# A macaron transformer block on one core: adaLN sums along k with outputs on partitions, x also transposed by the host, a first phase in passes of k-tiles, weights laid out in long runs

## What is computed

```python
mod = silu(c) @ w_ada + b_ada                 # c: [1, D], w_ada: [D, 9 D]
sh1, sc1, gt1, sh2, sc2, gt2, sh3, sc3, gt3 = split(mod, 9)
u = rmsnorm(x, norm1_g) * (1 + sc1) + sh1
h = x + 0.5 * gt1 * swiglu(u, ffn1_w_in, ffn1_w_out)      # D -> 2 x 5632 -> D
u = rmsnorm(h, norm2_g) * (1 + sc2) + sh2
h = h + gt2 * mixer(u)                        # windowed attention + mLSTM, w_in, w_att_up, w_mlstm_up, w_out
u = rmsnorm(h, norm3_g) * (1 + sc3) + sh3
h = h + 0.5 * gt3 * swiglu(u, ffn2_w_in, ffn2_w_out)
out = rmsnorm(h, final_g)
```

## Time and profile before

| | us |
|---|---|
| median of 3 runs | 2054.93 |
| lowest, highest | 2054.68, 3204.81 |
| span of the profiled execution | 2052.8 |
| TensorE busy in it | 2030.3 (99%) |
| VectorE busy | 1735.4 (85%) |
| ScalarE busy | 1195.1 (58%) |
| DMA, mean over the span | 263 GB/s |

### The profile page before, as it was taken

How to read it: one execution, slowest core, us unless ns; L and a number is a source line. 1 busy time by engine, 2 the same in 40 slices (tenths; PEclk the granted TensorE clock), 3 DMA queues, 4 the chain that set the end, 5 groups by cost and what they waited for, 6 DMA issues and landing times.

```text
span 2052.8 us, 24243 instructions
## 1 busy us (share of the span) xinstructions
PE 2030.3 (99%) x9197; PEld 1674.2 (82%) x9197; DVE 1735.4 (85%) x2038; ACT 1195.1 (58%) x1668; POOL 4.5 (0%) x22
## 2 busy tenths in 40 slices
PE   7999999999999999999999999999999999999998
PEld 6888888888888888888777888888888888888887
DVE  6998998888889898887998898988778777787786
ACT  4667444655346565446545666567775477755764
POOL 0000000000000000000000000000000000000000
PEclk9999999999999999999999999999999999999999
DMA  9998899998999778985666687565565556565554
GB/s 371 387 387 321 328 334 338 343 336 315 327 341 336 269 261 326 334 299 181 218 217 211 230 298 278 204 216 195 186 240 191 202 185 204 206 205 192 177 200 149
DMA packets 249572, 540.80 MB, mean 263 GB/s; under 512 B 11888, under 2 KB 14320, under 8 KB 248688
## 3 DMA queue, kind: packets, MB, share of 16 engines
q1 hardware_dynamic: 248368, 539.11, 74.1%
q10 hardware_dynamic: 1088, 0.15, 0.0%
HBM read 537.10 MB, written 2.11 MB: 263 GB/s over the span
## 4 chain that ended last, share of the span: by engine, by line
PE 94%; DMA 2%; DVE 2%; issue 1%; ACT 0%; SPq 0%; ACTq 0%; DVEq 0%
PE pb L909 13%; PE pb L917 13%; PE pa L909 13%; PE pb L913 13%; PE pa L917 13%; PE pa L913 12%; PE pa L1064 2%; PE pa L1058 2%; PE pa L1061 2%; DMA raw<-in_ffn_w_in_dram 1%; PE pa L1228 1%; PE pb L1219 1%; PE pb L1224 1%; PE pb L1228 1%; PE pa L1219 1%; PE pa L1224 1%
## 5 line engine op out<-in xcount | busy, mean ns | idle before, releaser
L1494 ACT CAST hi<-raw 128x1024 fp32r<-128x1024 f32 (+2 forms) x662 | 682.2, 1035 | 704.8 <-PE pb L917 316.3
L2105 DVE TENSOR_TENSOR lo<-raw,hi 128x1024 fp32r<-128x1024 f32 (+2 forms) x662 | 784.0, 1199 | 230.5 <-ACT hi L1494 228.0
L2205 DVE SCALAR_TENSOR_TENSOR ada_acc<-ada_w,cond,ada_acc 128x1024 f32<-128x1024 f32 (+1 forms) x210 | 236.7, 1127 | 6.3
L909 PE MATMUL pa<-hi,act_hi 128*128 128x512 f32 x816 | 226.4, 394 | 0.0
L909 PE MATMUL pb<-hi,act_hi 128*128 128x512 f32 x816 | 221.0, 393 | 0.0
L917 PE MATMUL pb<-lo,act_hi 128*128 128x512 f32 x816 | 218.2, 389 | 0.0
L917 PE MATMUL pa<-lo,act_hi 128*128 128x512 f32 x800 | 217.8, 389 | 0.0
L913 PE MATMUL pb<-hi,act_lo 128*128 128x512 f32 x800 | 214.0, 389 | 0.0
L913 PE MATMUL pa<-hi,act_lo 128*128 128x512 f32 x736 | 200.3, 389 | 0.0
L917 PEld LDWEIGHTS pb<-lo,act_hi 128*128 128x128 f32 x816 | 153.2, 188 | 32.0
L909 PEld LDWEIGHTS pb<-hi,act_hi 128*128 128x128 f32 x816 | 151.8, 188 | 32.7 <-issue 2.2
(11 more groups left out here) (482 smaller groups left out, 2622.1 us busy)
## 6 DMA issues: line engine op xcount, KB each, us to landing
raw<-in_ffn_w_in_dram SPq DMA_DIRECT2D x155, 1024.0 KB, 5.4
ada_w<-in_w_ada_dram SPq DMA_DIRECT2D x207, 512.0 KB, 6.4
raw<-in_w_in_dram SPq DMA_DIRECT2D x63, 1024.0 KB, 5.3
raw<-in_ffn_w_out_dram SPq DMA_DIRECT2D x60, 1024.0 KB, 5.2
ada_s<-in_w_ada_dram SPq DMA_DIRECT2D x64, 512.0 KB, 11.6
pair<-in_ffn_w_in_dram SPq DMA_DIRECT2D x20, 1024.0 KB, 6.7
raw<-in_ffn_w_out_dram SPq DMA_DIRECT2D x24, 768.0 KB, 4.5
raw<-in_w_out_dram SPq DMA_DIRECT2D x16, 1024.0 KB, 5.1
```

Of the source, the lines that this page charges most:

```text
L909: pe.matmul(bank[:, tt, cols], a_hi[:, k0 + kk, tok], w_hi[:, kk, cols], start=start and kk == 0, stop=False, skip_group_check=on)
L1494: act.copy(hi_of(ph, i, j, half)[:, 0:n, 0:w], raw_of(ph, i, j)[:, 2 * half:2 * half + n, 0:w])\
L2105: dve.tensor_tensor(lo_of(ph, i, j)[:, s, 0:w], raw_of(ph, i, j)[:, s, 0:w], hi_of(ph, i, j, half)[:, 0:n, 0:w].bitcast(F32), ALU.subtract)\
L2205: ins = dve.scalar_tensor_tensor(out=acc, in0=wt, scalar=cond[:, kt:kt + 1], in1=acc, op0=ALU.mult, op1=ALU.add)
```

## The change

The host lays out the inputs anew: each weight matrix in blocks of 512 columns, so that one chunk gives every partition one run of 8 KB (2 KB before); ffn1_w_in again in the order of the first phase (`w_first`); w_ada transposed, [output on partitions, k]; x also transposed (`x_t`); c, the norms and b_ada as columns (`cols`).

**adaLN.** cond is spread over all partitions as a row (16 small matmuls, four copies by DVE). A tile is [128 outputs, k], and one instruction multiplies it by the row and sums along k (`accum_out`). A k-tile's shift and scale need two products of 2048 columns. All flushes, folds and sums on PE go (`start_flush`, `fold_rows`, `gate_sums`). Gate rows, GT1 too in four quarters, go through DRAM.

**First phase.** In passes over k-tiles (0, 1), (2, 3), (4 to 7), (8 to 11), (12 to 15). A pass has two halves: two groups g that stay in their banks from the pass before, then the other two. Four sets of banks: pa, pb, px, pq. x comes transposed; DVE multiplies by gain and the row of reciprocal roots (`start_mod`), ACT adds the shift to get act_hi. In ffn1_out0 the chunks come in forward order, and its gate tiles stand 2 to a chunk.

```diff
+PASSES = ((0, 1), (2, 3), (4, 5, 6, 7), (8, 9, 10, 11), (12, 13, 14, 15))
+def first_chunks():
+    out = []
+    for p, kts in enumerate(PASSES):
+        one, two = ((0, 1), (2, 3)) if p % 2 == 0 else ((2, 3), (0, 1))
+        if p < 3:
+            out += [(p, 0, [(kt, g, ab) for g in one for ab in (0, 1)]) for kt in kts]
+        else:
+            out += [(p, 0, [(kt, g, ab) for ab in (0, 1) for kt in kts[k:k + 2]]) for k in (0, 2) for g in one]
+        if p < 2:
+            out += [(p, 1, [(kt, g, ab) for ab in (0, 1) for kt in kts]) for g in two]
+        else:
+            out += [(p, 1, [(kt, g, ab) for kt in kts]) for g in two for ab in (0, 1)]
+    return out
...
-    ada_plan("ffn1_out0", [2, 1, 2, 1] * 4)
+    ada_plan("ffn1_out0", [2] * 11 + [1, 1, 0, 0, 0])
...
+    NEW = {kt: min(u for u in range(64) if kt in [b[0] for b in first_unit_of(u)[2]]) for kt in range(KD)}
+    S_AT = {0: (0, 0), 1: (1, 2), 2: (6, 7), 3: (8, 9), 4: (13, 14), 5: (16, 17), 6: (18, 19), 7: (20, 21),
+            8: (27, 28), 9: (29, 30), 10: (32, 33), 11: (34, 35), 12: (43, 44), 13: (45, 46), 14: (48, 49), 15: (50, 51)}
...
+            def load_start(kt):
+                for m in (SC1, SH1):
+                    k = 2 * kt + (m == SH1)
+                    if k >= S_RING:
+                        sp.wait_ge(s_dve, k - S_RING + 1)
+                    sp.dma_start(ada_s[:, k % S_RING, :], w_ada[m * KD + kt, :, :]).then_inc(ada_s_in[k % S_RING], 16)
...
+            sp.dma_start(c_in[:, :], c).then_inc(c_ok, 16)
+            for tt in range(TT):
+                sp.dma_start(h[:, tt, :], x[:, tt, :]).then_inc(x_in[tt], 16)
+            for pos in range(32):
+                ahead = pos + (pos >= 12)
+                while loaded < KD and NEW[loaded] // 2 <= ahead:
...
+                    load_start(loaded)
+                    loaded += 1
+                load(plan["ffn1_in0"], 0, pos, w_first[pos], 4)
                 load_ada(plan["ffn1_in0"].c0 + pos)
...
+                cond_rows()
+                keep_busy(8)
+                rstd_row()
+                keep_busy(24)
+                pe.wait_ge(cond_row_ok, 4)
+                pe.wait_ge(rs_ok, 1)
+                for u in range(64):
+                    if u == 57:
+                        pe.wait_ge(pa_free, 2)
+                        transposes(0)
+                    if u in (60, 63):
+                        nb = (u - 57) // 3
+                        pe.wait_ge(nat_lo, 2 * nb)
+                        transposes(nb)
+                    first_unit(ph, u)
...
+                def keep(p, g, ab, after):
+                    act.wait_ge(unit_used, after + 1)
+                    act.copy(part[:, g, ab, :, :], bank[:, :, :]).then_inc(part_ok if p > 0 else bank_ok, 1)
+                    if p > 0:
...
+                        act.copy(bank[:, :, :], part[:, other, ab, :, :]).then_inc(bank_ok, 1)
...
-                            ins = dve.scalar_tensor_tensor(out=acc, in0=wt, scalar=cond[:, kt:kt + 1], in1=acc,
-                                                           op0=ALU.mult, op1=ALU.add)
+                    dve.scalar_tensor_tensor(out=wt, in0=wt, scalar=1.0, in1=cond_row[:, half * ADA_W:(half + 1) * ADA_W],
+                                             op0=ALU.mult, op1=ALU.mult, accum_out=macc[:, half, col:col + 1])\
...
+            def start_tile(kt, m):
+                k = 2 * kt + (m == SH1)
+                dve.wait_ge(ada_s_in[k % S_RING], 16 * (k // S_RING + 1))
+                wt = ada_s[:, k % S_RING, :]
+                dve.scalar_tensor_tensor(out=wt, in0=wt, scalar=1.0, in1=cond_row[:, :], op0=ALU.mult, op1=ALU.mult,
+                                         accum_out=macc[:, 0, m * KD + kt:m * KD + kt + 1]).then_inc(s_dve, 1)
+            def start_mod(kt):
...
+                dve.tensor_tensor(mod[:, sh], macc[:, 0, sh], bada[:, sh], ALU.add)
+                dve.scalar_tensor_tensor(out=gain[:, kt:kt + 1], in0=macc[:, 0, sc], scalar=sc_bias[:, kt:kt + 1],
+                                         in1=par[:, PAR["g1"] + kt:PAR["g1"] + kt + 1], op0=ALU.add, op1=ALU.mult)\
+                    .then_inc(s_mod, 1)
...
+                dve.scalar_tensor_tensor(out=n_t[:, kt, :], in0=n_t[:, kt, :], scalar=gain[:, kt:kt + 1],
+                                         in1=rs_row[:, :], op0=ALU.mult, op1=ALU.mult).then_inc(x_t_ok, 1)
+            def start_lo(kt):
...
+                for u in range(64):
+                    for kt in range(KD):
+                        if S_AT[kt][0] == u and kt > 0:
+                            start_tile(kt, SC1)
+                        if S_AT[kt][1] == u:
+                            start_tile(kt, SH1)
+                            start_mod(kt)
+                    for kt in range(KD):
+                        if NEW[kt] == u:
+                            start_lo(kt)
...
                     split(ph, 0, u // 2, u % 2, 2)
```

More of the change, by code:

```diff
@@ L123, in build, with tile_col @@
     SH1, SC1, GT1, SH2, SC2, GT2, SH3, SC3, GT3 = range(9)
[L124 to L140, removed]
+    HALF_ROWS = [(GT1, q) for q in range(4)] + [(m, half) for m in (SH2, SC2, GT2, SH3, SC3, GT3) for half in (0, 1)]
+    ROWS_OUT = (GT1, GT2, GT3)
+    ROW_TILES = [8 if m == GT1 else 16 for m, _ in HALF_ROWS]
+    TILES = [(row, sub) for row in range(len(HALF_ROWS)) for sub in range(ROW_TILES[row])]
+    def tile_col(t):
+        row, sub = TILES[t]
+        m, part_ = HALF_ROWS[row]
+        return m * KD + part_ * (ROW_TILES[row] // 2) + sub // 2, sub % 2
     n_tiles = {}
@@ L177, in build @@
             ring_of[t] = (ring is gates_tiles, k % size, k // size, ring[k - size] if k >= size else None)
[L178 to L184, removed]
@@ L208, in s_used, with mod_after, mod_count @@
-    def s_used(q, n):
-        on_dve = sum(kt not in ON_PE[x // KD] for x in range(KD * q + n) for kt in (x % KD,))
-        return on_dve, KD * q + n - on_dve
+    MODS = [(GT1, q) for q in range(4)] + [(m, 1) for m in (SH2, SC2, GT2, SH3, SC3, GT3)]
+    def mod_after(t):
+        row, sub = TILES[t]
+        return HALF_ROWS[row] if sub == ROW_TILES[row] - 1 and HALF_ROWS[row] in MODS else None
+    def mod_count(m, part_=1):
+        return MODS.index((m, part_)) + 1
+    S_RING = 4
+    FIRST = first_chunks()
@@ L602, in tile_in @@
             return (gate_in if late else ada_in)[slot], turn
-        def tile_sum(row, w):
-            return gate_acc[:, 0:w] if HALF_ROWS[row][0] == GT3 else ada_acc[:, row % 2, 0:w]
         def over(eng, n, body):
@@ L987, in gate_sums @@
[L987 to L997 removed]
+                    pe.transpose(px[:, 0, 0:P], ident[:, :], ident[:, :])
@@ L1145, in out_phase @@
                     for j, half, k0, n in units(4, kn):
-                        if gate1 and (b, j, half) in ((0, 1, 0), (1, 2, 1), (3, 0, 1)):
-                            gate_sums((b - b // 2,))
                         if b == 0 and k0 <= 4 * (kn - 1) < k0 + n:
@@ L1225, in first_unit @@
                               start=False, stop=False, skip_group_check=True)
                 pe.wait_ge(lo_done, u + 1)
-                for kk, tt, tok in places:
-                    mm = pe.matmul(bank[:, tt, :], act_hi[:, k0 + kk, tok], w_lo[:, 2 * half + kk, 0:NC],
-                                   start=False, stop=half == 1 and kk == 1, skip_group_check=True)
+                for m, tt, tok in places:
+                    mm = pe.matmul(bank(m)[:, tt, :], act_hi[:, blocks[m][0], tok], w_lo[:, s0 + m, 0:NC],
+                                   start=False, stop=True, skip_group_check=True)
```

884 lines of the change are left out of this document (298 added, 586 removed).

## The result

| | before | after |
|---|---|---|
| median of the runs, us | 2054.84 | 2068.93 |
| lowest to highest, us | 2054.68 to 3204.81 | 2067.52 to 2069.97 |
| ratio, 95% interval | | 1.0068, 1.0053 to 1.0083 |
| span of the profiled execution, us | 2052.8 | 2066.4 |
| start of the first-phase stream, us | 36.20 | 19.55 |

A forecast was written before the change was run, and what follows sets the result against it. TensorE bounds the kernel; 18.8 start + 174.1 units + 2.7 transposes + 12.5 waits end the phase at 208.1, 9.65 earlier; with 3.8 saved behind it, span 2039.4, time 2041.5 us, range 2031 to 2055.

The forecast's parts named there:

- slow clock at the start: At the new stream's start: a slow clock hides in the first waits, at most 1 us more.
- first k-tiles: TensorE's waits on VectorE early in the first phase: 3.5 us at k-tile 1, another 1 at k-tile 3.
- bunch at units 13 to 22: VectorE's bunched work, 34 us against 27.2 of PE, lead at most 7.8: between 0 and 6.8, taken as 5.
- bunch at 27 to 36: The same VectorE bunch one pass later begins with a full lead, so TensorE waits only 0.5 us.
- bunch at 43 to 52: VectorE's bunch with two or three gate tiles on top, 36 us against 27.2: 2 us of waits.
- The product's price: VectorE's accumulating product of 2048 columns takes 2.2 us, the sum being free.
- rival of half rate: Accumulating product with two SBUF sources runs at half rate, 4.3 us per 2048 columns: about 2165 us; chance 0.06.
- The rate: Transfers in the first phase run at 417 GB/s with 8 KB runs, taken from the loads of x.
- floor from w_first[25]: 65.5 MB up to that first-phase weight chunk land by 160 us at 417 GB/s, just ahead of PE.
- 3.8 us saved: After the first phase: four gate_sums go, 2.2 us, and 16 fold matmuls go, 1.6 us.
- Hidden; at worst 1 us each: Gate-row stores in 4-byte elements: 2.6 to 10.9 us of queue, covered by weights issued three chunks (16 us) ahead.
- a wait I have not seen (stores, a late bank, a cold clock): Rival, place not worked out: an unforeseen wait brings the time to 2055 to 2096 us; chance 0.06.

The follow-up runs named there:

- clock_kept_warm: The changed kernel with 54 filler transposes in place of 24 before the first-phase stream; phase end 220.84 against 221.03, span 2069.6 us.
- spread_products_again: Against gt1_on_pe: products of k-tiles 4 to 15 further apart and earlier, their tiles loaded one to three chunks earlier; median 2047.91 us, ratio 0.9966 to before.
- gt1_on_pe: The changed kernel with GT1 spread by small TensorE matmuls and ScalarE copies instead of through DRAM; base of most follow-ups; 2057.58 us, span 2055.8.
- quarter_products: Against gt1_on_pe: the 32 products for shift 1 and scale 1 take only the first 512 of 2048 columns; phase ends at 212.82, span 2047.1 us.
- gt1_16_byte_runs: The changed kernel with each GT1 quarter stored as 128 runs of 16 bytes instead of 512 single elements; 2055.51 us, span 2053.8.
- gt1_late_read: The changed kernel with SyncE reading each GT1 quarter back two chunks later, stores unchanged; span 2073.6 us, 7.2 worse.

## Why the prediction was wrong, point by point

The forecast's end of the phase was 208.1, measured 221.03. By its terms, the measured ones from where each of the 64 units starts in PE's timeline (a unit without a loss takes 2.72 us there, as forecast):

| term | forecast | measured |
|---|---|---|
| start of the stream | 18.8 | 19.55 |
| 64 units | 174.1 | 174.1 |
| transposes | 2.7 | 2.8 |
| slow clock at the start | hidden | 2.9 |
| first k-tiles | 4.5 | 1.6 |
| bunch at units 13 to 22 | 5 | 6.7 |
| bunch at 27 to 36 | 0.5 | 7.0 |
| bunch at 43 to 52 | 2 | 6.4 |
| bank hand-over at the end | 0.5 | 0 |

**The start** was right within a microsecond, and so the first gain of the change was real: 16.65 us. **The first k-tiles** and the clock together are 4.5, as forecast: the clock did hide in the first waits, as said, and clock_kept_warm shows it (4.6 in the same units, with one slow stretch later). The forecast had read the clock from a matmul of 421 ns; that row is one of 112 columns, so its comparison with the 128 columns of 272 ns was loose, and the conclusion came out all the same.

**The step that failed in the phase** is the one that gave the later bunches 0.5 and 2: "the same bunch at 27 to 36 begins with a full lead". The sum of VectorE's work there (34 against 27.2 us) was right; the lead was not there. TensorE took 33.9, 34.2 and 33.6 us for the three bunches of ten units, where the forecast's sums for VectorE were 34, 34 and 36: almost nothing was absorbed. For the first bunch the 5 was a choice between 0 and 6.8, and 6.7 is its upper end. VectorE's timeline just before that bunch:

```profile
98.68 1.23 DVE L1962 TENSOR_TENSOR lo<-raw,hi 128x1024 fp32r<-128x1024 f32 x1 [4.27 <-ACT hi L1384]
102.37 2.29 DVE L1991 SCALAR_TENSOR_TENSOR ada_s<-ada_s,cond_row 128x2048 f32<-128x2048 f32 x1 [2.46 <-DMA ada_s<-in_w_ada_dram]
```

It stands 4.3 us for ScalarE's hi, which is queued behind the bank copies of the pass (the cost that the forecast had named for units 12 to 15 and not carried to the next pass), and 2.5 us for a tile that was issued at 92.5, right behind x_t's last piece, as the first of four in a row. 6.7 of the 7.8 us of lead are gone before the first product. After it the split for unit 27 ends at 105.81, 0.2 us before TensorE takes it, and that for unit 28 is late:

```profile
110.05 1.20 PE L1144 MATMUL px<-lo,act_hi 128*128 128x512 f32 x4 [1.18 <-DVE lo L1962]
```

spread_products_again confirms the place: the losses at units 27 to 36 and 43 to 52 fall from 13.0 us in the base to 1.1, while a new one of 4.4 stands at units 23 and 24 (the wait of 2.56 us with its slow clock). That the bank copies are what ate the lead is read from the timelines; no run takes them away.

**The product's price** was right: 128x2048 with accumulator takes 2.29 us, the next instruction starts 2.21 later (80.14), the accumulator's read of 0.08 lies beside what follows. The rival of half rate fell:

```profile
77.93 2.28 DVE L2001 SCALAR_TENSOR_TENSOR ada_s<-ada_s,cond_row 128x2048 f32<-128x2048 f32 x1
80.14 0.08 DVE L2001 DVE_READ_ACCUMULATOR ada_s<-ada_s,cond_row 128x1 f32 x1
```

(These rows are of gt1_on_pe.) The forecast's rival of half rate, the third in its list, drew on the Trainium skill, "Vector Engine (DVE) Microarchitecture Reference", Points that are easy to get wrong: two non-bf16 SBUF sources halve the throughput, since no port is left for the accumulator's readback. Both sources are 32-bit in SBUF here, and against the form without accumulator nothing is halved: 1.22 us per 1024 columns with it, 1.28 without. Whether bf16 sources would be faster no run here shows.

**The rate** was right while transfers were asked for (420 against 417), and quarter_products kept 417 up to 100 us. The overhead per packet that the Trainium skill states ("DMA: Bandwidth & Descriptors", Why small descriptors are slow) would have given 400, an estimate by its 3 cycles; the measured gain is 8%, and the measurement decides. But the forecast's floor from w_first[25] took the rate to last until 160 us, and from 60 us on the queue ran dry (342 to 387), since chunks and tiles wait for their rings.

**Behind the phase** the 3.8 us saved were right (gt1_on_pe). **The second step that failed**, about as large for the total as the first, is "Hidden; at worst 1 us each" for the gate rows' stores. Three parts of it were wrong. The bounds of 20 to 85 ns a packet came from a small load and from large transfers, not from small writes, and held no case in which other packets are held up to 3.3 us. The sum was made for the 2048 elements of GT2 and GT3, which indeed cost nothing, and was passed on to GT1's quarters, whose stretch has DMA saturated with two gate tiles a chunk. And of the wait ahead of the read-back nothing was said: SyncE stands 5.7 to 10.1 us there with weights behind it. Measured: 11.4 us, the difference to gt1_16_byte_runs behind the phase.

In sum: 12.9 us in the phase and 14.1 behind it, against 208.1 and −3.8, are the 27 us by which the forecast span of 2039.4 was short of 2066.4. Of the rivals, "a wait I have not seen (stores, a late bank, a cold clock)" named the stores and the clock, without working out the place of either, and had the time in its range (2055 to 2096) at a chance of 0.06. That range was wide and rested on no sum, so its hit is luck.

## What to carry to other kernels

A lead that is to absorb a bunch must be read off at the bunch's start, again in every pass: list what the feeding engine and queue do in the 10 us before it. The same work, with products and their tiles spread more evenly, was worth 10 us here and needed no new instruction. A row that must change from partitions to a line goes over TensorE (0.81 us for 512 values) rather than through DRAM in 4-byte elements next to a saturated weight stream.

## What the hardware did that was not expected

- A DRAM store of 512 elements of 4 bytes landed 12.6 to 15.5 us after its issue, and 4 KB packets beside it took 3.3 us each in place of 0.16, at a busy share of 0.88. With the same 2 KB in 128 pieces of 16 bytes it landed in about 9 us, and TensorE's waits in ffn1_out0 fell from 10.3 to 1.0 us.
- Shares near 1.0 do not mean throughput: 262 to 266 us has 0.88 with 17 GB/s. The two must be read together.
- Granted clock: it stayed at 1.00 after the single waits of 1.2 us in the phase. After waits of 2.49 (28.84 in clock_kept_warm), 3.75 and 4.12 us, matmuls of 512 columns came every 0.43 us instead of 0.227 for 3 to 7 us, which is the 1.2 GHz level, and 1.4 to 2.9 us were lost beside the wait. But the length of one wait does not settle it: after 3.48 us (263.50 in gt1_late_read) and 2.12 us (300.42 in the changed kernel) the clock stayed, and after 1.33 us (177.85 in clock_kept_warm, 1.14 us of waiting 2.5 us before it) it fell.
- 8 KB runs brought 421 GB/s from 20 to 100 us in spread_products_again, at a share of 1.01 to 1.02, where the 2 KB runs of the kernel before brought 387 at 1.05.
